# Where the split weights begin in SBUF: 96 bytes past a multiple of 128, in every stage

## The chip, the cores and the metric

The kernel runs on one core of a Trainium2 chip, one of the chip's eight. The metric is the device time in microseconds (us), the median of three runs. TensorE is called PE in the profile (its weight loads PEld), VectorE DVE, ScalarE ACT, GpSimd POOL and SyncE SP. SBUF is the on-chip memory from which TensorE reads both operands of a matmul; every tile has 128 partitions, and "address" below means the byte offset within a partition.

## The reference

One layer of a streaming encoder, over 256 tokens of 2048 features, all in float32. Cut to what matters:

```
x = x + hybrid_mixer(rmsnorm(x), w_in, ..., w_br, w_out)
x = x + memory_cross_attention(rmsnorm(x), rmsnorm(mem), xa_wq, xa_wkv, xa_wo, ...)
x = x + (silu(g) * u) @ ffn_down      # g, u = split(causal_conv3(rmsnorm(x) @ ffn_up))
```

The mixer has one wide input projection (h @ w_in), three token mixers (gated DeltaNet, mLSTM, stick-breaking attention), a projection of each by w_br, gates, and an output projection by w_out. Nearly all of the work is the dense products of 256 tokens with 367 MB of weights that are read once each.

## The kernel before, in words

A float32 product is made from three products of the faster type float32r. A weight w is split into hi = round(w) and lo = w - hi, the activations x likewise, and the product is hi·x_hi + hi·x_lo + lo·x_hi.

**Units.** The weights come as 177 units (`STREAM`), each of 256 output columns: 2048 x 256 values, or 1408 x 256 in the down projection (`DN`). SP loads a unit into one of two slots of `raw`. Each unit is handled in two halves. For each half ScalarE writes `w_hi` (`hi_half`, shown as L540), VectorE writes `w_lo` (`lo_half`, L1131), and TensorE multiplies (`half_unit`). `w_hi_home` and `w_lo_home` have two slots, one for each half, of 2048 + 64 float32r values (8448 bytes, 66 times 128). ScalarE may overwrite a slot once TensorE has used it (`half_used`), and TensorE waits for `lo_ready`.

**The kinds of stage**, which differ in what TensorE holds and what it streams:
- Feature-major (`FM`, and the branch projections `BR`): the held operand (stationary, loaded by LDWEIGHTS) is a 128 x 128 block of weights, and the streamed one (moving) is 256 tokens of activations. `three` issues three matmuls for each of 16 blocks: L1961, L1962, L1963.
- Token-major (`TM_`: stages BV, CV, V): the other way around. The held operand is a block of activations and the streamed one is 256 columns of weights. The same three lines.
- Up and down projection (`UP`, `DN`): weights are held. One matmul streams x_hi and x_lo together (two rows of 256, shown as 128x512; L1998 and L2473), and a second one streams x_hi against w_lo (L2000, L2474). Two matmuls for each block.

In the profile a matmul reads `bank<-moving,stationary`: `bank<-x_home,w_hi_home` holds weights, `bank<-w_hi_home,x_home` streams them. The type float32r is shown as f32 there. A matmul's weight load is the LDWEIGHTS instruction of the same line; the load for the next matmul runs beside the present one.

**Addresses.** Tiles lie one behind another in SBUF, in the order of the code. In the built program the homes begin at these addresses: `w_hi_home` 49280, `w_lo_home` 66176, `x_home` 83072, `act_hl` 130464, `mem_hl` 146848, `y_hl` 196000, `gw_hi` 196768, `gw_both` 204960. Taken modulo 128, both weight homes and `x_home` begin at 0, and all the others at 32. The kernel itself begins the activations 8 values (32 bytes) into `x_home`:

```
x_hl = x_home[:, 8:8 + 2 * KC * SEQ].rearrange("p (j k s) -> p j k s", j=2, k=KC)
```

Every step from one block to the next (512 or 1024 bytes, 8448 between slots) is a multiple of 128, so an operand keeps its place modulo 128 through a stage. This is what TensorE reads, in bytes past a multiple of 128:

| matmuls | moving | stationary | moving minus stationary |
|---|---|---|---|
| feature-major, branches, UP, DN (before) | 32 | 0 | 32 |
| token-major (before) | 64 | 32 | 32 |
| the small gate projection, L2119 and L2120 | 32 | 32 | 0 |

The gate projection multiplies the ten gate columns that belong to no unit: 32 matmuls on `gw_both` and `gw_hi`, of the same type and shape as the others (a 128 x 128 stationary operand, 256 columns moving), once at the start:

```
mm(bank[4][:, 0:SEQ], gw_both[:, k, :], x_hl[:, 0, k, :], start=k == 0, stop=False)
last = mm(bank[4][:, 0:SEQ], gw_hi[:, k, :], x_hl[:, 1, k, :], start=False, stop=k == KC - 1)
```

The order of the instructions on each engine is written out by hand, and semaphores join the engines.

Of the kernel before, what the change touches and what calls it, by code (L numbers as in the profile page):

```python
# [8 lines left out]
P = 128  # L9
SEQ, D = 256, 2048  # L10
TT = SEQ // P
KC = D // P
# [7 lines left out]
CW = 256  # L20
GDN_TAPS, FFN_TAPS = 4, 3
EPS = 1e-6
BIG = 1e30


C_A = 0
# [78 lines left out]
def shape_masks():  # L105
# [8 lines left out]
    incl = np.concatenate([r <= t, r <= c], 1)  # L114
    return np.concatenate([ident, upper, later] + levels + [np.where(strict, 0, -BIG), np.where(incl, 0, BIG)],
                          1).astype(np.float32)


def build_program(nc, T, out):
# [3 lines left out]
    with ctx:  # L123
        def sb(name, shape, dt=f32, stack=ctx):
            return stack.enter_context(nc.sbuf_tensor(name, shape, dt))
# [5 lines left out]
        raw = sb("raw", [P, 2, KC * CW])  # L131
        w_hi_home = sb("w_hi_home", [P, 2, KC * P + 64], f32r)
        w_lo_home = sb("w_lo_home", [P, 2, KC * P + 64], f32r)
        w_hi, w_lo = w_hi_home[:, :, 0:KC * P], w_lo_home[:, :, 0:KC * P]
        wt_hi, wt_lo = w_hi_home[:, :, 16:16 + KC * P], w_lo_home[:, :, 16:16 + KC * P]
        e_scope = ExitStack()
        x_back = sb("x_back", [P, KC, SEQ], f32, e_scope)
        o_tm = sb("o_tm", [P, TT, D], f32, e_scope)
# [257 lines left out]

        def split_out(tile, kind, half):
            if kind == TM_:
                return (wt_hi if tile is w_hi else wt_lo)[:, half, :]
            k = DG if kind == DOWN else KC  # L400
            return tile[:, half, 0:k * P].rearrange("p (k n) -> p k n", n=P)

# [125 lines left out]
        def up_bank(par, half):  # L528

            return bank[4 + 2 * par + half]  # L530
# [7 lines left out]
        def _(act):  # L538
# [3 lines left out]
            def hi_half(name, i, par, hp, half):  # L542

                act.wait_ge(raw_full[par], hp * 16 + 16)
                if not (isinstance(hp, int) and 2 * hp + par == 0):
                    act.wait_ge(half_used, hp * 4 + (2 * par + half - 1))
                copy(split_out(w_hi, kind_of[name], half), halves(raw, kind_of[name], half, par)).then_inc(hi_ready, 1)

            def hi_part(part, name, i, par, hp, half):

                if part == 0:
                    act.wait_ge(raw_full[par], hp * 16 + 16)
                    if name != "A":
                        act.wait_ge(half_used, hp * 4 + (2 * par + half - 1))
                ks = slice(part * (KC // 2), (part + 1) * (KC // 2))
                copy(split_out(w_hi, FM, half)[:, ks, :], halves(raw, FM, half, par)[:, ks, :]).then_inc(hi_ready if part else wp_h, 1)
# [135 lines left out]
            def first_weights(j, done):  # L692
                act.wait_ge(*((raw_full[0], 16) if j else (w0_in, 16)))
                ks = slice(j * (KC // 2), (j + 1) * (KC // 2))
                copy(split_out(w_hi, FM, 0)[:, ks, :], halves(raw, FM, 0, 0)[:, ks, :]).then_inc(done, 1)
# [1260 lines left out]
        def _(pe):  # L1956
            mm = nc.tensor.matmul

            def three(o, w, x, start, stop):

                mm(o, w[0], x[0], start=start, stop=False)  # L1961
                mm(o, w[0], x[1], start=False, stop=False)  # L1962
                return mm(o, w[1], x[0], start=False, stop=stop)  # L1963
# [14 lines left out]
            def half_unit(name, i, par, hp, half, acts, ready=None, passed=None, parts=None, ks=range(KC)):  # L1978

                kind = kind_of[name]  # L1980
                whole = hp * 4 + (2 * par + half + 1)
                pe.wait_ge(*((wp_l, parts) if parts else (lo_ready, whole)))
                if kind == TM_:
                    for k in range(KC // 2):
                        kk = half * (KC // 2) + k
                        w = [t[:, half, k * CW:(k + 1) * CW] for t in (wt_hi, wt_lo)]
                        for a in range(TT):
                            x = [acts[:, j, kk, a * P:(a + 1) * P] for j in range(2)]
                            last = three(bank[par + 2 * a][:, 0:CW], x, w, kk == 0, kk == KC - 1)
                else:  # L1990
                    cuts = (0, GH, GH + MH, KC) if kind == BR else (0, KC)
                    for k in range(KC if name == "UP" else 0):
                        if parts and k == KC // 2:
                            pe.wait_ge(lo_ready, whole)
                        if ready and k % ready[2] == 0:
                            pe.wait_ge(ready[0], ready[1] + k // ready[2] + 1)
                        o = up_bank(par, half)
                        mm(o[:, :].rearrange("p (j s) -> p j s", j=2), w_hi[:, half, k * P:(k + 1) * P], acts[:, :, k, :],  # L1998
                           start=k == 0, stop=False)
                        last = mm(o[:, SEQ:2 * SEQ], w_lo[:, half, k * P:(k + 1) * P], acts[:, 0, k, :], start=False, stop=k == KC - 1)  # L2000
                    for k in ks if name != "UP" else ():
                        if parts and k == KC // 2:
                            pe.wait_ge(lo_ready, whole)
                        if ready and k % ready[2] == 0:
                            pe.wait_ge(ready[0], ready[1] + k // ready[2] + 1)
                        g = sum(k >= c for c in cuts) - 1
                        w = [t[:, half, k * P:(k + 1) * P] for t in (w_hi, w_lo)]
                        last = three(bank[par + 2 * g][:, half * SEQ:(half + 1) * SEQ], w, [acts[:, j, k, :] for j in range(2)],
                                     k == cuts[g], k + 1 == cuts[g + 1])
                        if kind == BR and half and k + 1 in cuts[1:3]:  # L2010
                            last.then_inc(br_t, 1)
                        if passed is not None and k % 2 and k + 1 < KC:
                            last.then_inc(passed, 1)
                if ks[-1] == KC - 1:
                    last.then_inc(half_used, 1)

            def product_half(m, acts=x_hl, ready=None, passed=None, parts=None, ks=range(KC)):

                name, i, par, hp, half = half_of(m)
                if half == 0 and ks[0] == 0:  # L2020
                    wait_bank(name, i)
                half_unit(name, i, par, hp, half, acts, ready, passed, parts, ks)

            def project(name, acts, start=0, stop=None):
                def unit(i, par, hp):
                    wait_bank(name, i)
                    for half in range(2):
                        half_unit(name, i, par, hp, half, acts)

                stop = COUNT[name] if stop is None else stop  # L2030
                if start < 2:
                    each_unit(pe, name, unit, start, min(2, stop))
                each_unit(pe, name, unit, max(2, start), stop)
# [59 lines left out]
            for k in range(KC):  # L2093
# [8 lines left out]
                w = [t[:, 0, k * P:(k + 1) * P] for t in (w_hi, w_lo)]  # L2102
# [424 lines left out]
```

## Time and profile before

| | |
|---|---|
| median of 3 runs | 2003.33 us (2003.0 to 2004.33) |
| profiled execution, first to last instruction (span) | 2001.0 us |
| what the median has beyond that span | 2.3 us |
| PE busy | 1987.1 us (99%), 14790 matmuls |
| PE weight loads busy | 1895.9 us (95%) |
| DVE busy | 1216.1 us (61%) |
| ACT busy | 892.0 us (45%) |
| granted TensorE clock | 1.000 of full speed |

The page gives no time of the profiled execution apart from its span, so the sums are made against the span and the 2.3 us are added. Matmuls overlap in the pipeline: the duration in a row is that of one matmul from start to end, longer than the distance from one start to the next. The distance between starts, called the pace below, sets the time of a long run of matmuls. It is read from the first and last start of a group, or from start times in the timeline.

### The profile page before, as it was taken

The page shows a single profiled execution, that of the slowest core. Times are in us where ns is not written, and L with a number is a line of the kernel's source. Part 1 is how long each engine was busy: PE and PEld are TensorE (multiplying, and loading weights), DVE is VectorE, ACT ScalarE, POOL GpSimd, SP SyncE. Part 2 cuts the span into 40 slices and gives each one's busy share as a digit, 9 for nine tenths or more (in the row PEclk, how much of TensorE's full clock was granted, in tenths as well). Part 3 has the DMA queues.
Part 4 walks back from the last instruction along what each step waited for, and adds up shares of the span by engine and source line. Part 5 has one row for each costly group of instructions (what it writes and reads, how often), then busy time and mean ns, then how long its engine had stood idle before and what let it go on. Part 6 is the DMA issues. An engine that isn't in the chain of part 4 may idle for free.

```text
span 2001.0 us, 34706 instructions
## 1 busy us (share of the span) xinstructions
PE 1987.1 (99%) x14790; PEld 1895.9 (95%) x14790; DVE 1216.1 (61%) x1352; ACT 892.0 (45%) x877; POOL 40.5 (2%) x62
## 2 busy tenths in 40 slices
PE   8999999999999999999999999999999999999999
PEld 8999999999999999999999999988888888888888
DVE  5677645445454476576655345777777777754444
ACT  5445334434364343455434344544444444433333
POOL 1000100000000000000000000000000000000000
PEclk9999999999999999999999999999999999999999
DMA  8766754665557766565564456665656565566664
GB/s 268 220 192 195 226 159 143 198 200 166 182 174 247 243 198 223 169 194 186 178 199 129 139 168 198 212 208 171 207 171 206 173 204 174 177 205 223 185 203 134
DMA packets 356637, 382.65 MB, mean 191 GB/s; under 512 B 8144, under 2 KB 351604, under 8 KB 355124
## 3 DMA queue, kind: packets, MB, share of 16 engines
q1 hardware_dynamic: 350947, 353.36, 55.9%
q0 software_dynamic: 5584, 27.70, 4.0%
q8 instruction: 88, 1.44, 0.3%
q14 instruction: 18, 0.14, 0.0%
HBM read 367.47 MB, written 13.58 MB: 190 GB/s over the span
## 4 chain that ended last, share of the span: by engine, by line
PE 97%; DVE 1%; ACT 1%; DMA 0%; issue 0%; SPq 0%; DVEq 0%; ACTq 0%
PE bank L1961 18%; PE bank L1962 18%; PE bank L1963 18%; PE bank L1998 16%; PE bank L2000 8%; PE bank L2473 8%; PE bank L2474 4%; PE bank L2381 1%; PE bank L2400 1%; PE bank L2158 1%; DVE w_lo_home L1131 1%; ACT w_hi_home L540 0%; PE bank L2204 0%; PE bank L2061 0%; PE bank L2152 0%; DMA ident<-in_shape_masks 0%
## 5 line engine op out<-in xcount | busy, mean ns | idle before, releaser
L1131 DVE TENSOR_TENSOR w_lo_home<-raw,w_hi_home 128x2048 fp32r<-128x2048 f32 (+1 forms) x349 | 756.7, 2168 | 606.2 <-ACT w_hi_home L540 605.8
L540 ACT ACTIVATE w_hi_home<-raw 128x2048 fp32r<-128x2048 f32 (+2 forms) x359 | 645.0, 1798 | 1047.5 <-PE bank L1963 624.3
L1961 PE MATMUL bank<-x_home,w_hi_home 128*128 128x256 f32 x2304 | 648.1, 281 | 1.9 <-DVE w_lo_home L1131 1.9
L1962 PE MATMUL bank<-x_home,w_hi_home 128*128 128x256 f32 x2304 | 643.1, 279 | 0.0
L1963 PE MATMUL bank<-x_home,w_lo_home 128*128 128x256 f32 x2304 | 642.8, 279 | 0.0
L1998 PE MATMUL bank<-x_home,w_hi_home 128*128 128x512 f32 x1408 | 488.5, 390 | 0.1
L1961 PEld LDWEIGHTS bank<-x_home,w_hi_home 128*128 128x128 f32 x2304 | 433.1, 188 | 2.8 <-DVE w_lo_home L1131 1.4
L1962 PEld LDWEIGHTS bank<-x_home,w_hi_home 128*128 128x128 f32 x2304 | 433.2, 188 | 0.2
L1963 PEld LDWEIGHTS bank<-x_home,w_lo_home 128*128 128x128 f32 x2304 | 433.0, 188 | 0.0
L2000 PE MATMUL bank<-x_home,w_lo_home 128*128 128x256 f32 x1408 | 397.0, 282 | 0.0
L1998 PEld LDWEIGHTS bank<-x_home,w_hi_home 128*128 128x128 f32 x1408 | 264.2, 188 | 55.7 <-issue 0.4
L2000 PEld LDWEIGHTS bank<-x_home,w_lo_home 128*128 128x128 f32 x1408 | 266.1, 189 | 0.0
L2473 PE MATMUL bank<-act_hl,w_hi_home 128*128 128x512 f32 x704 | 245.2, 391 | 0.0
L2474 PE MATMUL bank<-act_hl,w_lo_home 128*128 128x256 f32 x704 | 198.5, 282 | 0.0
L2473 PEld LDWEIGHTS bank<-act_hl,w_hi_home 128*128 128x128 f32 x704 | 132.2, 188 | 27.6
L2474 PEld LDWEIGHTS bank<-act_hl,w_lo_home 128*128 128x128 f32 x704 | 133.1, 189 | 0.0
L1961 PE MATMUL bank<-w_hi_home,mem_hl 128*128 128x256 f32 x256 | 73.5, 287 | 0.0
L1865 DVE SCALAR_TENSOR_TENSOR tmp<-tmp,vec 128x254 f32<-128x254 f32 (+1 forms) x176 | 73.0, 476 | 0.0
L1961 PE MATMUL bank<-mem_hl,w_hi_home 128*128 128x256 f32 x256 | 71.8, 280 | 0.0
L1962 PE MATMUL bank<-mem_hl,w_hi_home 128*128 128x256 f32 x256 | 71.5, 279 | 0.0
L1962 PE MATMUL bank<-w_lo_home,mem_hl 128*128 128x256 f32 x256 | 71.5, 279 | 0.0
L1961 PE MATMUL bank<-y_hl,w_hi_home 128*128 128x256 f32 x256 | 71.5, 279 | 0.0
(315 smaller groups left out, 1942.4 us busy)
## 6 DMA issues: line engine op xcount, KB each, us to landing
raw<-in_w_in SPq DMA_DIRECT2D x52, 2048.0 KB, 8.4
raw<-in_ffn_up SPq DMA_DIRECT2D x44, 2048.0 KB, 8.0
raw<-in_ffn_down SPq DMA_DIRECT2D x32, 1408.0 KB, 6.6
raw<-in_xa_wkv SPq DMA_DIRECT2D x16, 2048.0 KB, 9.3
raw<-in_w_br SPq DMA_DIRECT2D x8, 2048.0 KB, 8.4
raw<-in_w_out SPq DMA_DIRECT2D x8, 2048.0 KB, 8.3
raw<-in_xa_wq SPq DMA_DIRECT2D x8, 2048.0 KB, 8.3
raw<-in_xa_wo SPq DMA_DIRECT2D x8, 2048.0 KB, 8.4
```

Source lines behind the costliest of these rows:

```text
L540: return nc.scalar.activation(out_, in_, func, **kw)
L1131: tt(split_out(w_lo, kind, half), halves(raw, kind, half, par), split_out(w_hi, kind, half).bitcast(f32), ALU.subtract).then_inc(lo_ready, 1)
L1865: ins = v.scalar_tensor_tensor(o, b, w, o, ALU.mult, ALU.add)
L1961: mm(o, w[0], x[0], start=start, stop=False)
L1962: mm(o, w[0], x[1], start=False, stop=False)
L1963: return mm(o, w[1], x[0], start=False, stop=stop)
L1998: mm(o[:, :].rearrange("p (j s) -> p j s", j=2), w_hi[:, half, k * P:(k + 1) * P], acts[:, :, k, :], start=k == 0, stop=False)
L2000: last = mm(o[:, SEQ:2 * SEQ], w_lo[:, half, k * P:(k + 1) * P], acts[:, 0, k, :], start=False, stop=k == KC - 1)
L2158: last = mm(o[:, i * P:(i + 1) * P], lhs(n), rhs(n), start=True, stop=True)
L2381: last = mm(mb(j)[:, 0:SEQ], qT[:, 4 * h + c, a * P:(a + 1) * P], kT[:, 4 * h + c, :], start=c == 0, stop=c == XC - 1)
L2473: mm(o[:, :].rearrange("p (j s) -> p j s", j=2), w_hi[:, half, k * P:(k + 1) * P], x, start=g + k == 0, stop=False)
L2474: last = mm(o[:, SEQ:2 * SEQ], w_lo[:, half, k * P:(k + 1) * P], x[:, 0, :], start=False, stop=g * DG + k == FC - 1)
```

## The change

The first value of every split-weight slot moves. In feature-major stages, branches, UP and DN, `w_hi` and `w_lo` began at 0 bytes of their slot; in token-major stages (`wt_hi`, `wt_lo`) at 64 bytes. Now all begin at 24 values, which is 96 bytes.

```
+W_AT = 24
...
-        w_hi, w_lo = w_hi_home[:, :, 0:KC * P], w_lo_home[:, :, 0:KC * P]
-        wt_hi, wt_lo = w_hi_home[:, :, 16:16 + KC * P], w_lo_home[:, :, 16:16 + KC * P]
+        w_hi, w_lo = (t[:, :, W_AT:W_AT + KC * P] for t in (w_hi_home, w_lo_home))
...
             if kind == TM_:
-                return (wt_hi if tile is w_hi else wt_lo)[:, half, :]
+                return tile[:, half, :]
...
-                        w = [t[:, half, k * CW:(k + 1) * CW] for t in (wt_hi, wt_lo)]
+                        w = [t[:, half, k * CW:(k + 1) * CW] for t in (w_hi, w_lo)]
```

The slots have room for it (24 + 2048 of 2112 values), no tile moves, and each engine's list of instructions is the same, row by row. What TensorE reads after the change, in bytes past a multiple of 128:

| matmuls | moving | stationary | moving minus stationary |
|---|---|---|---|
| feature-major, branches, UP, DN | 32 | 96 | -64, that is 64 modulo 128 |
| token-major | 96 | 32 | 64 |
| the gate projection | 32 | 32 | 0 |

## Rows read from the trace of the kernel before

**Rows 1.** The page's first part: engines, busy time, share, instructions.

```profile
PE 1987.1 (99%) x14790; PEld 1895.9 (95%) x14790; DVE 1216.1 (61%) x1352; ACT 892.0 (45%) x877; POOL 40.5 (2%) x62
```

**Rows 2.** Waits of PE, 20 to 1990 us: total, times, longest.

```profile
PE bank L1961 <- DVE w_lo_home L1131: 1.9, 3, 1.2
```

**Rows 3.** Waits of all engines, the whole span.

```profile
ACT w_hi_home L540 <- PE bank L1963: 624.3, 187, 6.4
DVE w_lo_home L1131 <- ACT w_hi_home L540: 605.8, 274, 7.2
```

**Rows 4.** Groups by line and shape: count, then busy us, mean ns of one, idle before.

```profile
L1961 PE MATMUL bank<-x_home,w_hi_home 128*128 128x256 f32 x2304 | 648.1, 281 | 1.9 <-DVE w_lo_home L1131 1.9
...
L1961 PE MATMUL bank<-w_hi_home,mem_hl 128*128 128x256 f32 x256 | 73.5, 287 | 0.0
L1961 PE MATMUL bank<-mem_hl,w_hi_home 128*128 128x256 f32 x256 | 71.8, 280 | 0.0
...
L1961 PE MATMUL bank<-y_hl,w_hi_home 128*128 128x256 f32 x256 | 71.5, 279 | 0.0
...
L1961 PE MATMUL bank<-w_hi_home,x_home 128*128 128x256 f32 x160 | 44.7, 279 | 0.0
```

**Rows 5.** Tile w_hi_home: min/median/max ns, first and last start us.

```profile
L1961 PE MATMUL bank<-y_hl,w_hi_home x256: 277/279/281, 684.2 to 773.4; 128*128 128x256 f32 x128
...
L1998 PE MATMUL bank<-x_home,w_hi_home x1408: 390/390/579, 1259.9 to 1748.9; 128*128 128x512 f32 x176
...
L2473 PE MATMUL bank<-act_hl,w_hi_home x704: 390/390/484, 1749.3 to 1996.2; 128*128 128x512 f32 x176
```

**Rows 6.** Timeline of PE, token-major, at 540 us: start us, duration us.

```profile
539.79 0.28 PE L1962 MATMUL bank<-w_lo_home,x_home 128*128 128x256 f32 x1
...
540.61 0.28 PE L1963 MATMUL bank<-w_hi_home,x_home 128*128 128x256 f32 x1
```

**Rows 7.** Timeline of PE, the gate projection, at 38 us.

```profile
37.83 0.28 PE L2120 MATMUL bank<-x_home,gw_hi 128*128 128x256 f32 x1
37.95 0.28 PE L2119 MATMUL bank<-x_home,gw_both 128*128 128x256 f32 x1
...
38.67 0.28 PE L2119 MATMUL bank<-x_home,gw_both 128*128 128x256 f32 x1
```

**Rows 8.** Tiles gw_both, then w_hi_home with y_hl, as in rows 5.

```profile
L2119 PEld LDWEIGHTS bank<-x_home,gw_both x16: 187/192/192, 36.2 to 39.7; 128*128 128x128 f32 x16
L2119 PE MATMUL bank<-x_home,gw_both x16: 278/283/283, 36.3 to 39.9; 128*128 128x256 f32 x16
...
L1961 PEld LDWEIGHTS bank<-y_hl,w_hi_home x256: 187/188/189, 684.1 to 773.3; 128*128 128x128 f32 x128
```

**Rows 9.** The longest pieces of the critical chain: start us, length us, what.

```profile
248.80 2.68 PE bank L2158 x24
...
1077.12 3.45 PE bank L2381 x16
```

**Rows 10.** Busy time in stretches: us, PE, PEld, DVE, ACT, POOL, clock, DMA.

```profile
700.00:750.00 50.00, 50.00 (x431) 50.00 (x431) 38.36 (x38) 20.42 (x14) 0.00 (x0) 1.00 0.62 196
1300.00:1400.00 100.00, 100.00 (x579) 88.67 (x578) 78.30 (x109) 44.07 (x45) 0.00 (x0) 1.00 0.59 189
37.20:39.60 2.40, 2.40 (x22) 2.40 (x21) 1.11 (x1) 1.25 (x1) 0.69 (x1) 1.00 1.08 372
```

**Rows 11.** Splitting, groups as in rows 4: first feature-major (700:760), then token-major (1060:1160).

```profile
L1131 DVE TENSOR_TENSOR w_lo_home<-raw,w_hi_home 128x2048 fp32r<-128x2048 f32 x11 | 25.2, 2289 | 13.0 <-ACT w_hi_home L540 13.0
...
L540 ACT ACTIVATE w_hi_home<-raw 128x2048 fp32r<-128x2048 f32 x11 | 21.1, 1918 | 35.4 <-PE bank L1963 35.4
...
L1131 DVE TENSOR_TENSOR w_lo_home<-raw,w_hi_home 128x2048 fp32r<-128x2048 f32 x13 | 29.7, 2286 | 16.6 <-ACT w_hi_home L540 16.6
...
L540 ACT ACTIVATE w_hi_home<-raw 128x2048 fp32r<-128x2048 f32 x13 | 24.9, 1913 | 47.3 <-PE bank L1963 47.3
```

## The prediction, made before the changed kernel ran

> **What bounds the kernel now.** I read the page's busy times first [rows 1]: TensorE is busy for 1987.1 of 2001.0 us, so only 13.9 us hold no matmul. Then the waits. From 20 to 1990 us TensorE waits for VectorE 1.9 us in all [rows 2], while ScalarE waits 624.3 us for TensorE to free a slot, and VectorE 605.8 us for ScalarE [rows 3]. So the splitting engines and the transfers have room, and the time is that of a row of matmuls. The granted clock is full in every stretch [rows 10], 2.4 GHz. What is left to change is how far apart two matmuls start.
>
> I read that pace next. In the branch stage the L1961 matmuls on y_hl start at 684.2 us first and at 773.4 us last, 256 of them [rows 5]. Between two of them lie three matmuls, so the pace is 89.2 / (255 x 3) = 116.6 ns. Token-major gives 0.82 us over seven starts, 117 ns [rows 6]. In the up projection a pair (512 and 256 columns) takes 489.0 / 1407 = 347.5 ns [rows 5]. In the down projection a pair takes 246.9 / 703 = 351.2 ns, a few transposes and the joins between column blocks included.
>
> The gate projection has the same type and shape, and it is slower: 37.83 to 38.67 us for seven starts [rows 7], 120.0 ns. Its matmuls last 283 ns and its loads 192 ns in the median, where the ordinary ones take 279 and 188 ns [rows 5, 8]. The clock is 1.00 there too [rows 10]. What distinguishes it in layout: its stationary operand begins 32 bytes past a multiple of 128, as the moving one does. Feature-major and token-major differ in both absolute places (32 over 0, 64 over 32), agree in the difference of 32, and run at one pace within what the rows resolve. The price of a layout can be read here, but at two layouts only, and the new one (difference 64) is neither.
>
> How much of the pace could layout touch? Two rows bound it. Plain float32 matmuls of 128 columns with a fresh weight load each run at 2.68 us / 24 = 111.7 ns, and those of 256 columns at 3.45 / 16 = 215.6 ns [rows 9]. That float32 streams its columns in two passes is an inference from the second: 512 steps at 2.4 GHz are 213.3 ns. One pass of 256 steps takes 106.7 ns. So our 116.6 ns has some 10 ns beyond streaming and 5 ns beyond the pace of loads in the nearest row.
>
> A rule speaks against any effect. The Trainium skill (TensorE: Matmul & The Clock Gate, Step-by-step: what each phase is for) says that TensorE has two independent SBUF read ports, and that loading the next weights takes no read bandwidth from the running matmul. By it, where one operand lies relative to the other would not matter, and the sum would be zero. This trace does not agree plainly: 120.0 against 116.6 ns at equal shape, type and clock is not what independent reads would give, unless the gate projection is slow for another reason.
>
> **The change part by part.**
> - *Stationary reads, feature-major, branches, UP, DN:* from 0 to 96 bytes past 128. The three-matmul kinds hold 2304 + 256 + 256 blocks with weights stationary; the token-major ones 256 + 160 with activations stationary [rows 4]. These are 3232 blocks and 9696 matmuls, some 1131 us at 116.6 ns. UP and DN have 1408 + 704 pairs [rows 5], 4224 matmuls. Together 13920.
> - *Moving reads, token-major:* from 64 to 96, the same new difference of 64 (1248 of the matmuls above).
> - *ScalarE and VectorE writes and VectorE's read:* moved likewise. ScalarE takes 1918 ns at 0 bytes and 1913 ns at 64, VectorE 2289 and 2286 [rows 11]. Their start does not show in their duration. I take nothing for 96 bytes. Matmuls of a half last 48 x 116.6 ns = 5.6 us, which hides both (4.2 us in sequence, and they overlap with the half before). If the cover were gone, even 5 ns on each of about 350 splits of either engine would be 3.5 us.
> - *DMA, semaphores, order:* nothing changes.
>
> Price of one matmul at difference 64. No row shows it. The nearest row with another layout is the gate projection: +3.4 ns (120.0 - 116.6), about 8 cycles of 2.4 GHz. From below the row of float32 loads bounds it: 111.7 - 116.6 = -4.9 ns, or -68 us in all. From above the only row for reads that don't overlap at all is the load's own 188 ns [rows 8], which would be +71 ns and 990 us; I don't believe that end, as the slower layout costs 3.4 ns.
>
> I choose +3.4 ns for every split-weight matmul. My reason is an even-granule view: 32 bytes past a multiple of 64 appears to cost 8 cycles on either operand. Feature-major has one such operand (the moving), token-major one (the stationary), the gate projection two, at 120.0. After the change 96 is again 32 past 64, so every matmul has two. This view gives the two equal paces and the slower one without more assumptions. The sum: 9696 x 3.4 ns = 33 us, and for UP and DN 4224 x 3.4 ns = 14 us (one shifted load per matmul, whatever its length). Together 47 us on the span of 2001.0, with 2.3 us around it: 2050 us. I put 2049 us (rounding 8 cycles to 3.33 ns gives 46).
>
> **The rivals.**
> - *Faster: the two reads take turns, and the wait falls with the difference.* With difference 0 the pace is 288 cycles, with 32 it is 280; in line with that 64 would give 272, 113.3 ns. Price -3.3 ns x 13920 = -46 us: 1957 us. For it: the two kinds of stage agree in the difference and in nothing else, and it stays above the 111.7 ns. Against: two points make any line, and it decides only if the difference and not the absolute place counts. Half the effect, 1980 us, is possible where only some stages respond.
> - *No change.* The gate projection is slow for a reason of its own: it alternates two tiles and two halves of x instead of reusing a tile. Then 2003 us. The sixteen-byte lines of SBUF that the Trainium skill describes (SBUF — State Buffer, Door 1: The DMA port swizzle) would say the same, as 0, 32, 64 and 96 are all multiples of 16. No row here shows lines of that size.
> - *Much slower: the difference counts, and 64 is its worst place.* If the pace rises on both sides of 32 and 64 costs twice what 0 does, 16 cycles or 6.7 ns, then 13920 x 6.7 = +93 us: 2096 us. For it: 0 is worse than 32. Against: it needs a step between 32 and 64 that no row shows.
> - *Only the three-matmul stages slow:* +33 us, 2036 us; in UP and DN half of the long matmul runs with no load beside it. Kept within the forecast's own range.
>
> **How the numbers follow.** Forecast, with its variant of 2036: 0.43. Much slower: 0.11. No change: 0.18. Faster: 0.28. So slower by over 0.2% has 0.54, within 0.2% 0.18, faster by over 0.2% 0.28; 0.2% (4 us) is about what a measurement of this kernel tells from no change. The forecast's own range is 2030 to 2058. The range of 8 in 10 runs from 1954, which takes in the faster rival, to 2062; it leaves out the much slower one and what lies below 1954.
>
> **What would show it.** If right: L1961 matmuls on y_hl span 91.8 us from first to last instead of 89.2 (120.0 ns), their median duration is 283 ns and that of their loads 192 ns; token-major steps by 0.12 us; a pair in UP takes about 354 ns; the gate projection keeps 120.0; DVE and ACT keep their durations and wait longer for TensorE. If the pace in those rows is 113 ns, the turn-taking rival holds and I have the sign wrong; if 116.6, the gate projection misled me. A pace that moves in feature-major and not in token-major would say that the held operand's absolute place counts. A longer wait of TensorE for VectorE, with an equal pace, would say that the price lies in the splitting, which I have at nothing.

## The result, and the profile after

The changed kernel takes 2009.08 us, the median of five runs from 2004.10 to 2014.77, against 2003.82 us (2003.0 to 2004.48) before. The ratio is 1.0031, with a 95% interval of 1.0020 to 1.0041: slower by 0.3%. The forecast was 2049 us. The spread is a result as well. These five runs of the kernel before lie within 1.5 us (thirteen measured with the first experiments within 3.0), those of the changed one within 10.7 us. The profiled execution, to which all rows below belong, is the fastest of the five: 2004.1 us with a span of 2002.1 us, 1.1 us above the span before.

The small sum hides two large parts of opposite sign. These rows of the tile w_hi_home answer to [rows 5] and [rows 8]; the columns are min/median/max ns, then the first and last start in us.

```profile
L1961 PEld LDWEIGHTS bank<-y_hl,w_hi_home x256: 187/188/188, 679.2 to 765.9; 128*128 128x128 f32 x128
L1961 PE MATMUL bank<-y_hl,w_hi_home x256: 276/276/276, 679.3 to 766.0; 128*128 128x256 f32 x128
...
L1998 PE MATMUL bank<-x_home,w_hi_home x1408: 389/397/581, 1247.4 to 1745.5; 128*128 128x512 f32 x176
...
L2473 PE MATMUL bank<-act_hl,w_hi_home x704: 392/397/481, 1745.9 to 1997.3; 128*128 128x512 f32 x176
```

The branch stage has become faster: 86.7 us from first to last start against 89.2, which is 113.3 ns a matmul against 116.6. UP starts at 1247.4 us instead of 1259.9, so everything ahead of it has gained 12.5 us. From there to the last L2473 start it takes 749.9 us instead of 736.3, a loss of 13.6 us. A pair in UP takes 498.1 / 1407 = 354.0 ns (347.5 before), in DN 251.4 / 703 = 357.6 (351.2). The sum is +1.1 us, the difference of the spans.

Not all stages of three matmuls gained. This is the timeline of PE at 644 us, in stage GC of the changed kernel: start us, duration us.

```profile
643.70 0.28 PE L1961 MATMUL bank<-x_home,w_hi_home 128*128 128x256 f32 x1
...
644.88 0.28 PE L1962 MATMUL bank<-x_home,w_hi_home 128*128 128x256 f32 x1
644.99 0.28 PE L1963 MATMUL bank<-x_home,w_lo_home 128*128 128x256 f32 x1
...
646.57 0.36 PE L1961 MATMUL bank<-x_home,w_hi_home 128*128 128x256 f32 x1 [1.29 <-DVE w_lo_home L1131]
646.76 0.28 PE L1962 MATMUL bank<-x_home,w_hi_home 128*128 128x256 f32 x1
...
647.12 0.28 PE L1962 MATMUL bank<-x_home,w_hi_home 128*128 128x256 f32 x1
...
647.91 0.28 PE L1963 MATMUL bank<-x_home,w_lo_home 128*128 128x256 f32 x1
```

The same lines, the same operands and the same places in memory run at 1.29 / 11 = 117 ns up to 644.99 us, then TensorE waits 1.3 us for a late unit, and from 647.12 on they run at 0.79 / 7 = 113 ns. I followed the start times of all three-matmul stages in blocks of twelve. Nearly every block after the change has one of two paces, 113.3 ns (272 cycles of 2.4 GHz) or 117.8 ns (282.7 cycles). Which of the two is settled within some twelve matmuls after a break, that is, after TensorE has waited or done other matmuls. It then stays through hundreds of matmuls, and it is the same while VectorE splits and while it is idle (113.3 ns either way in the branch stage), so the writes into the slots don't set it. Before the change nine blocks in ten had 116.7 ns (280 cycles).

TensorE need not wait for the pace to change. Here token-major BV passes into feature-major BO at 424.75 us with no gap:

```profile
423.39 0.28 PE L1961 MATMUL bank<-w_hi_home,x_home 128*128 128x256 f32 x1
...
424.75 0.28 PE L1961 MATMUL bank<-x_home,w_hi_home 128*128 128x256 f32 x1
...
426.16 0.28 PE L1961 MATMUL bank<-x_home,w_hi_home 128*128 128x256 f32 x1
```

Twelve steps take 1.36 us, then 1.41: 113.3 and 117.5 ns. So the passage from one kind of stage to the other counts as a break too.

| matmuls of the three-matmul stages, in whole blocks | 113.3 ns | 116.7 ns | 117.8 ns |
|---|---|---|---|
| before | 0 | 8136 | 864 |
| changed, first profile | 5400 | 24 | 3540 |
| changed, second profile (below) | 2580 | 12 | 6432 |

(Four blocks to a half; a block counts where nothing else lies among its twelve matmuls, by the mean of their eleven start distances: up to 114.5, up to 117.3, up to 120 ns. Blocks above that hold a break.) In the first profile 5400 x 3.3 ns = 17.8 us are gained and 3540 - 864 matmuls lose 1.1 ns each, 2.9 us: 15 us, of which 12.5 arrived. The longer wait for VectorE below is 1.3 us of the rest.

The other predicted readings, in the order of the groups. Token-major, at 540 us, seven steps take 0.80 us (539.82 to 540.62), 114 ns. The wait of TensorE for VectorE from 20 to 1990 us is 3.2 us instead of 1.9 [rows 2]:

```profile
PE bank L1961 <- DVE w_lo_home L1131: 3.2, 3, 1.3
```

ScalarE waits less for the three-matmul stages, 604.0 us instead of 624.3 [rows 3]; I had forecast a longer wait:

```profile
ACT w_hi_home L540 <- PE bank L1963: 604.0, 184, 6.4
```

The windows, with the columns of [rows 10] (this is the row of UP, 1300 to 1400 us): the clock is as before, and in UP 569 matmuls touch the 100 us where 579 did. The gate projection and the splitting are unchanged [rows 8, 11]:

```profile
1300.00:1400.00 100.00, 100.00 (x569) 86.87 (x568) 76.75 (x105) 43.55 (x45) 0.00 (x0) 1.00 0.58 188
```

```profile
L2119 PE MATMUL bank<-x_home,gw_both x16: 283/283/283, 36.4 to 40.0; 128*128 128x256 f32 x16
```

```profile
L1131 DVE TENSOR_TENSOR w_lo_home<-raw,w_hi_home 128x2048 fp32r<-128x2048 f32 x12 | 27.5, 2289 | 13.7 <-ACT w_hi_home L540 13.7
```

### The profile page after: what moved, and what is told of

Its sections match the earlier page's. It is cut to its first block, busy times and chain, and to the rows that moved or that the text cites. A ratio compares the mean times of both kernels' runs of the same rounds, so it can differ in the third digit from the quotient of the medians.

```text
span 2002.1 us, 34706 instructions
## 1 busy us (share of the span) xinstructions
PE 1987.0 (99%) x14790; PEld 1880.8 (94%) x14790; DVE 1216.2 (61%) x1352; ACT 892.4 (45%) x877; POOL 40.4 (2%) x62
## 4 chain that ended last, share of the span: by engine, by line
PE 96%; DVE 2%; DMA 1%; ACT 1%; issue 0%; SPq 0%; DVEq 0%; ACTq 0%
PE bank L1961 18%; PE bank L1962 18%; PE bank L1963 18%; PE bank L1998 17%; PE bank L2000 8%; PE bank L2473 8%; PE bank L2474 4%; DMA raw<-in_w_in 1%; DVE w_lo_home L1131 1%; PE bank L2381 1%; PE bank L2400 1%; PE bank L2158 1%; ACT w_hi_home L540 0%; PE bank L2204 0%; PE bank L2061 0%
## 5 line engine op out<-in xcount | busy, mean ns | idle before, releaser
L540 ACT ACTIVATE w_hi_home<-raw 128x2048 fp32r<-128x2048 f32 (+2 forms) x359 | 645.3, 1799 | 1045.7 <-PE bank L1963 604.0
L1961 PE MATMUL bank<-x_home,w_hi_home 128*128 128x256 f32 x2304 | 646.3, 280 | 3.4 <-DVE w_lo_home L1131 3.2
L1998 PE MATMUL bank<-x_home,w_hi_home 128*128 128x512 f32 x1408 | 497.9, 398 | 0.0
L1961 PEld LDWEIGHTS bank<-x_home,w_hi_home 128*128 128x128 f32 x2304 | 435.3, 189 | 4.8 <-issue 2.9
L1998 PEld LDWEIGHTS bank<-x_home,w_hi_home 128*128 128x128 f32 x1408 | 264.7, 188 | 65.5 <-issue 0.2
L2473 PE MATMUL bank<-act_hl,w_hi_home 128*128 128x512 f32 x704 | 249.7, 398 | 0.0
L2473 PEld LDWEIGHTS bank<-act_hl,w_hi_home 128*128 128x128 f32 x704 | 132.4, 188 | 32.4
L1961 PE MATMUL bank<-w_hi_home,mem_hl 128*128 128x256 f32 x256 | 73.3, 286 | 0.0
L1963 PE MATMUL bank<-w_hi_home,mem_hl 128*128 128x256 f32 x256 | 71.3, 279 | 0.0
L1961 PE MATMUL bank<-mem_hl,w_hi_home 128*128 128x256 f32 x256 | 71.0, 277 | 0.0
L1963 PE MATMUL bank<-mem_hl,w_lo_home 128*128 128x256 f32 x256 | 70.7, 276 | 0.0
```

The costliest lines, as they stand in the source:

```text
L540: return nc.scalar.activation(out_, in_, func, **kw)
```

## The experiments

From here on a difference is the moving operand's address minus the stationary one's, in bytes, as a signed value modulo 256 (the homes of the weights begin 128 past a multiple of 256, all activations 160). Before: +32 everywhere. Changed: -64, and +64 in token-major stages. The expectations of the first two kernels and the first two maps count modulo 128. In a table of places, W_AT gives where a stage's weights begin, in columns of 4 bytes: with the activations at 32 bytes and the weights held, 0 is +32, 24 is -64. All kernels but the repeat of the changed one are the kernel before with a table of places, one for each stage, and keep its line numbers. Their tables are written in short form below, stages and then their place:

```
-        w_hi, w_lo = w_hi_home[:, :, 0:KC * P], w_lo_home[:, :, 0:KC * P]
-        wt_hi, wt_lo = w_hi_home[:, :, 16:16 + KC * P], w_lo_home[:, :, 16:16 + KC * P]
+        w_hi, w_lo, kind_of = w_hi_home, w_lo_home, {n: k for n, _, _, _, k in STREAM}
+        placed = lambda tile, name: tile[:, :, W_AT[name]:W_AT[name] + KC * P]
...
```

### One part at a time

```
+W_AT = 24 in every stage but UP and DN, 0 there
```

> Weights begin at 96 bytes in all stages of three matmuls, and again at 0 in the up and down projection. Theory D (the pace is set by moving minus stationary, modulo 128; at 64 a run of matmuls settles at either 113.3 or 117.8 ns and keeps that until it is broken): the pairs of UP and DN go back from 353.5 to 346.7 ns, which gives back 1408 x 6.8 + 704 x 6.8 = 14.4 us against the changed kernel, and the rest keeps the 13 us gained in its profiled execution or less: 1988 to 1999 us, varying from run to run by up to 10 us. Rival G (something in the whole program, for instance the transfers, takes back what the matmuls gain): 2003 us or more.

Measured: 1999.62 us, nine runs from 1995.84 to 2001.08; ratio to before 0.9972 (0.9962 to 0.9982). UP takes the old time, 489.0 us from first to last start of L1998:

```profile
L1961 PEld LDWEIGHTS bank<-y_hl,w_hi_home x256: 192/192/192, 677.7 to 767.8; 128*128 128x128 f32 x128
L1961 PE MATMUL bank<-y_hl,w_hi_home x256: 281/281/281, 677.8 to 767.9; 128*128 128x256 f32 x128
...
L1998 PE MATMUL bank<-x_home,w_hi_home x1408: 390/390/579, 1257.6 to 1746.6; 128*128 128x512 f32 x176
```

The branch stage, whose places are those of the changed kernel, has 90.1 us here, 117.8 ns. The duration of these loads tells the two paces apart as well: 192 ns here, 188 ns there. (It is one of the three loads of a block that lengthens, and not in every stage that of L1961.) Rival G falls, and the median lies just above the 1988 to 1999 us of theory D. The profiled execution is the slowest of the nine, 2001.08 us; it has 2676 matmuls at 113.3 ns and 6324 at 117.8.

```
+W_AT = 24 in UP and DN; elsewhere as before (0, token-major 16)
```

> The reverse: only UP and DN hold weights at 96 bytes, all the rest as before. Theory D: each pair takes 353.5 ns, +14.4 us, 2018 us, with no more variation from run to run than the kernel before, because the two-state stages are unchanged. Rival G: less than 10 us of it shows.

Measured: 2017.38 us (2016.70 to 2017.77), ratio 1.0067 (1.0053 to 1.0081), and L1998 spans 498.1 us. Theory D holds in both: the loss is 13.6 us (14.4 expected), and the spread is gone, 1.1 us. Rival G falls here too. UP and DN carry the whole loss, the other stages the gain and the spread.

### The same kernel once more

> The changed kernel once more, to see whether the two paces belong to places in the program or to the execution. Theory D: each unbroken run of matmuls settles anew, so other stages are at 113.3 and at 117.8 ns than in the first profile (there the branches ran at 113.3 and XO at 117.8), and the span differs by up to 10 us; UP and DN are at 353.4 ns a pair again. Rival C (the place in the program decides, for instance what runs before): the same stages at the same paces, and the branches at 113.3.

Measured: 2014.59 us in one run, span 2012.6 us.

```profile
L1961 PE MATMUL bank<-y_hl,w_hi_home x256: 281/281/281, 678.1 to 768.2; 128*128 128x256 f32 x128
...
L1998 PE MATMUL bank<-x_home,w_hi_home x1408: 392/397/581, 1257.8 to 1756.0; 128*128 128x512 f32 x176
```

The branch stage is at 117.8 ns in this execution. Everything ahead of UP has gained 2.1 us instead of 12.5, and UP and DN lose as in the first profile. Rival C falls as stated: the same place in the program can run at either pace. But the place has a large share in it. Z, BQK, BV and CV ran at 113.3 ns in all three profiles with these places, BO and XO at 117.8. Counted by halves, this profile and that of the kernel with UP and DN put back, taken on another chip, have the same pace in 196 of 200; the first profile agrees with this one in 120 of 199, and the others lie mostly from GB to V. What decides at a break, and how much of it is chance, stays open.

### Maps of places

Each map is one run of a kernel that gives each stage another place, and I read the pace of each stage from start times. As wholes the four maps took 2029.65, 2022.15, 2018.53 and 2008.75 us, one run each.

```
+W_AT = A 0, Z GA BV DN 8, BQK BO CQK UP 16, CV Q 24, GB GC 28, BR 20, WO 12, K 4, V 0, XO 26
```

> A map: each stage gets a place of its own for its weights, the activations stay at 32 bytes past 128. Differences (moving minus stationary, modulo 128): A 32; Z and GA 0; BV (token-major) 0; BQK, BO and CQK 96; CV (token-major) 64; GB and GC 48; BR 80; WO 112; K 16; Q 64; V (token-major) 96; XO 56; UP 96; DN 0. Theory D: GA, and BV with it, run at 120.0 ns like the gate projection; CV at 113.3 or 117.8; A at 116.7; K between 116.7 and 120. Rival P (each operand's own place counts, 32 past 64 costing 8 cycles): GA 120.0, but BQK, BO and CQK (64 stationary, 32 moving) 116.7, and V (0 moving, 32 stationary) 116.7. Rival N (the gate projection was slow for a reason of its own): GA at 116.7.

```
+W_AT = GA Q 0, CQK CV 8, A Z BV GB GC WO UP DN 16, BR 22, BQK BO K V XO 24
-        x_hl = x_home[:, 8:8 + 2 * KC * SEQ].rearrange("p (j k s) -> p j k s", j=2, k=KC)
+        x_hl = x_home[:, 0:0 + 2 * KC * SEQ].rearrange("p (j k s) -> p j k s", j=2, k=KC)
```

> The same kind of map with the activations of the feature-major stages at 0 instead of 32 bytes past 128. Differences: A and Z 64 (0 over 64); GA and Q 0 (0 over 0); BQK, BO 32 (0 over 96); BV 64 (64 over 0); CQK 96; CV 32 (32 over 0); GB and GC 64 (0 over 64); BR 72; WO 64; K and V 64 (as in the changed kernel); XO 32; UP 64 (0 over 64); DN 96. Theory D: GA and Q at 120.0 ns though both operands begin at a multiple of 128; BQK, BO, XO and CV at 116.7; A, Z, GB, GC, WO at 113.3 or 117.8, and a pair in UP at 353.5. Rival P: GA and Q are the fastest, 113.3 ns, as nothing is off a multiple of 64, and so are A, GB and WO, always.

```
+W_AT = XO 24, A GA WO V UP 32, CQK K 40, BV Q 48, Z BQK BO CV GB GC BR DN 56
```

> A map to find what the difference is taken modulo of, activations at 32 past 128 (all 160 past a multiple of 256; the weight homes begin 128 past 256). Differences in bytes, moving minus stationary, given as signed values modulo 256: A, GA, WO and UP -96; Z, BQK, BO, GB, GC, BR, DN +64 (weights at 224 of the slot, before only -64 was run); CQK and K 128; BV -96; CV -64; Q +96; V +96; XO -64 (control). Theory D128 (only modulo 128 counts): A, GA, WO at 116.7 ns and pairs of UP at 346.7, since -96 is 32 modulo 128; CQK and K at 120.0; Z to BR at 113.3 or 117.8; pairs of DN 353.4. Theory D256 (the difference counts modulo 256 or more; the map with x at 0 had -96 in BQK, BO and XO at 117 to 119 and not at 116.7): A, GA, WO at 117 to 119, UP at 353.4, CQK and K not at 120.0.

```
+W_AT = A Z BQK BO CV GB GC WO Q UP 0, BR 2, DN 6, GA XO 8, BV CQK 24, K V 56
-        x_hl = x_home[:, 8:8 + 2 * KC * SEQ].rearrange("p (j k s) -> p j k s", j=2, k=KC)
+        x_hl = x_home[:, 16:16 + 2 * KC * SEQ].rearrange("p (j k s) -> p j k s", j=2, k=KC)
```

> A map with the activations of the feature-major stages at 64 past 128. Signed differences modulo 256: A, Z, BQK, BO, GB, GC, WO, Q and UP +64 (64 over 0); GA and XO +32 (64 over 32, weights held); BV +32 (96 over 64); CQK -32; CV -64; BR +24; K +64; V -64; DN +8. Theory D: GA and XO run at 116.7 ns as at 32 over 0. +64 is like -64 if only the distance counts: 113.3 or 117.8, and 353.4 for a pair in UP. Rival S (the sign counts: the moving read ahead of the load by 64 goes on from what +32 does to 0): +64 at 113.3 ns always and pairs in UP below 346.7.

What the four maps and the kernels above gave, by difference:

| difference | ns a matmul (stages of three) | where (moving over stationary, modulo 128) |
|---|---|---|
| 0 | 120.0 | GA, Z, BV (32 over 32); GA, Q (0 over 0) |
| +16 | 117 to 120 | K (32 over 16) |
| +24 | 117.5 to 118 | BR (fourth map) |
| +32 | 116.7, at times 117.8 | 32 over 0, 64 over 32, 32 over 0 token-major |
| +64, -64 | 113.3 or 117.8 | 0 over 64, 64 over 0, 96 over 32, 32 over 96 and others |
| +96 | 120.0 | Q, V |
| 128 | 118 to 120 | CQK, K |
| -96 | 117 to 119, a part of WO 120.0 | A, GA, WO, BV (32 over 0); BQK, BO, XO (0 over 96) |
| -80 to -16, without -64 | 118 to 119, a part of WO 120.0 | GB, GC, XO, BR, BQK, CQK, WO, V |

Two rows each of the timeline of PE decide between theories: in the first map Z (32 over 32), in the second Q (0 over 0), in the fourth XO (64 over 32).

```profile
133.82 0.28 PE L1961 MATMUL bank<-x_home,w_hi_home 128*128 128x256 f32 x1
...
134.78 0.28 PE L1963 MATMUL bank<-x_home,w_lo_home 128*128 128x256 f32 x1
```

```profile
999.83 0.28 PE L1963 MATMUL bank<-x_home,w_lo_home 128*128 128x256 f32 x1
...
1000.79 0.28 PE L1962 MATMUL bank<-x_home,w_hi_home 128*128 128x256 f32 x1
```

```profile
1199.76 0.28 PE L1963 MATMUL bank<-x_home,w_lo_home 128*128 128x256 f32 x1
...
1200.69 0.28 PE L1962 MATMUL bank<-x_home,w_hi_home 128*128 128x256 f32 x1
```

Eight steps take 0.96 us in the first two, 120 ns, and 0.93 in the third, 116 ns. So:
- Rival N falls: ordinary matmuls at difference 0 run at 120.0 ns. The gate projection was a true sample; with the activations at 0 or 64 it runs at 117.0 itself.
- Rival P, which is the view my forecast rested on, falls: with both operands at a multiple of 128 the pace is 120.0 ns, the slowest, and not the fastest.
- Theory D holds in what it says of the difference: 64 over 32 is as 32 over 0, and 0 over 0 as 32 over 32. It falls in the modulus. -96 and +32 are equal modulo 128, but GA at -96 takes 117 to 119 ns. The difference counts modulo 256 at least. No larger modulus shows: the two halves of a unit lie 8448 bytes apart, which is 256 modulo 512, and run alike (GA of the first map at 120.0 ns in both halves, the branch stage of the kernel before at 116.6).
- Rival S falls: +64 has the same two paces as -64.

For the pairs of UP and DN the maps follow another pattern. The table has the mean inside a half, without the joins that the 347.5 ns of [rows 5] include:

| | hi, lo difference | ns a pair, UP or DN |
|---|---|---|
| before, e1 | +32, +32 | 346.7 |
| third map, UP | -96, -96 | 346.7 |
| fourth map, UP | +64, +64 | 349.0 |
| third map, DN | +64, +64 | 352.4 |
| fourth map, DN | +8, +8 | 351.7 |
| changed, e2 | -64, -64 | 353.3 |
| first map | UP -32, DN 0 | 352.9, 353.4 |
| second map | UP -64, DN -32 | 353.3, 353.3 |

(e1 is the kernel with UP and DN put back, e2 the one with only these two changed.) The third map's UP has the old time, 1271.5 to 1760.5 us. There theory D256, which holds for the stages of three matmuls, missed and D128 was right; in the fourth map UP at +64 took 349.0 ns, where theory D had 353.4:

```profile
L1998 PE MATMUL bank<-x_home,w_hi_home x1408: 391/392/584, 1271.5 to 1760.5; 128*128 128x512 f32 x176
```

### High and low halves apart

A second table places `w_lo`:

```
+        placed = lambda tile, name: (lambda at: tile[:, :, at:at + KC * P])((W_LO if tile is w_lo else W_AT)[name])
+(W_AT, W_LO) = A GA CV WO DN (24, 0), Z GC V (24, 16), BQK CQK Q UP (0, 24),
+               BV BO GB K (24, 56), BR (24, 8), XO (56, 24)
```

> The high and the low halves of the weights get places of their own, written (hi, lo) as signed moving minus stationary in bytes: A, GA, WO (-64, +32); Z, GC (-64, -32); BQK, CQK, Q (+32, -64); BV (+64, -64 with 224 of 256); BO, GB, K (-64, +64); CV (+64, -32); BR (-64, 0); V (+64, +32); XO (+64, -64); UP (+32, -64); DN (-64, +32). Theory B (what counts is the load that runs beside a matmul, against what this matmul streams): in UP the load of lo runs beside the matmul of 512 columns, so UP (+32, -64) shows 235 + 118 ns, as with both at -64; in DN the load of lo lies at +32 and the long matmul takes 228, while the load of hi beside the short one lies at -64 and costs nothing, 346.7 a pair. Rival A (each matmul's own operands count, whatever loads beside it): the other way around, UP 228 + 118 and DN 235 + 118. In the stages of three matmuls I have no number for mixtures: between 113.3 and 118; if one of them holds 113.3 ns after every break, it is the version to time.

```profile
L1998 PE MATMUL bank<-x_home,w_hi_home x1408: 388/393/586, 1266.5 to 1755.5; 128*128 128x512 f32 x176
L2473 PE MATMUL bank<-act_hl,w_hi_home x704: 392/396/481, 1755.9 to 2005.7; 128*128 128x512 f32 x176
...
L1961 PE MATMUL bank<-mem_hl,w_hi_home x256: 276/276/468, 872.8 to 960.0; 128*128 128x256 f32 x128
```

One run, 2012.58 us. Theory B falls: UP has the old time, 489.0 us, with its low halves at -64, and DN (high halves at -64) is slow, 351.1 ns a pair. Among the mixtures one stands out. High at -64 with low at +64 gave 113.3 ns in BO, GB and K, in every block away from a break (in K the L1961 matmuls on mem_hl span 87.2 us, in the kernel before 89.9 by the same view). The reverse in XO gave 118.9, and no other mixture came below 116.7.

```
+(W_AT, W_LO) = every feature-major and branch stage (24, 56); BV CV V (24, 24); UP DN (0, 0)
```

> From the map of places for hi and lo apart: the high halves at 96 bytes, the low ones at 224 (24 and 56 values; differences -64 and +64) in all feature-major and branch stages; both at 96 in the token-major stages; both at 0 in UP and DN. In the map BO, GB and K with these places ran at 113.3 ns after every break. If this holds elsewhere (theory L: with the low halves 128 bytes further on, the 117.8 state can't be kept), some 8300 feature-major matmuls gain 3.3 ns, 27 us, and the token-major ones up to 4 us: 1974 to 1980 us with little variation. If the three stages had luck (theory R: two states as before), 1990 to 2000 us, varying. Where TensorE runs faster than the weights come, a few us go to waits for them.

Measured: 1976.43 us, four runs from 1976.03 to 1978.45, against 2003.66 (2003.31 to 2004.11); ratio 0.9867 (0.9851 to 0.9884). The span of the profiled execution is 1973.9 us.

```profile
L1961 PE MATMUL bank<-y_hl,w_hi_home x256: 276/276/276, 669.3 to 756.0; 128*128 128x256 f32 x128
...
L1961 PE MATMUL bank<-mem_hl,w_hi_home x256: 276/276/468, 848.1 to 935.4; 128*128 128x256 f32 x128
L1961 PE MATMUL bank<-w_hi_home,mem_hl x256: 276/279/468, 1024.6 to 1143.7; 128*128 128x256 f32 x128
...
L1998 PE MATMUL bank<-x_home,w_hi_home x1408: 390/390/579, 1232.9 to 1722.0; 128*128 128x512 f32 x176
```

All feature-major and branch stages run at 113.3 ns after every break. UP starts 27.0 us earlier than before, at 1232.9 us, and UP and DN take the old time. Only V, token-major and with both halves at +64, still has the two paces (119.1 us, 118.9 in the kernel before). Theory L holds for the feature-major and branch stages. This kernel is 1.3% faster than the kernel before, by the medians 1.6% faster than the changed one, and its four runs lie within 2.4 us.

```
+the same, with UP (0, 56), DN (0, 24), BV CV V (56, 24)
```

> The kernel with 96 and 224 bytes once more, with other places in four kinds of stage, (hi, lo) as signed moving minus stationary: UP (+32, +64), DN (+32, -64), token-major V, BV and CV (-64, +64). If each matmul's own operands count in the pairs, as UP (+32, -64) at 346.7 ns and DN (-64, +32) at 351 said, both UP and DN are at 346.7 here; if the load beside the long matmul counts, at 353.4. Token-major: no number, 113.3 if the mixture of signs does there what it does feature-major. The feature-major stages again at 113.3 (theory L) or in two states (theory R).

```profile
L1961 PE MATMUL bank<-x_home,w_hi_home x2304: 276/276/469, 16.7 to 1235.4; 128*128 128x256 f32 x192
...
L1998 PE MATMUL bank<-x_home,w_hi_home x1408: 388/397/579, 1235.8 to 1733.7; 128*128 128x512 f32 x176
L2473 PE MATMUL bank<-act_hl,w_hi_home x704: 388/393/481, 1734.1 to 1980.9; 128*128 128x512 f32 x176
```

One run, 1987.65 us. Feature-major stages are at 113.3 ns again, a second execution. The token-major ones ran at 117.8 ns. The pairs did not follow either rule: UP (+32, +64) took 353.0 ns, DN (+32, -64) 346.7. That "each matmul's own operands count" is thereby refuted for UP, and what sets a pair's pace stays open.

## Why the prediction was wrong

- **What bounds the kernel, and that the pace depends on the places: right.** Clock, order, splitting and transfers did not change; the price is in the distance between matmul starts, and the gate projection was a fair sample of another layout [rows 7]. Its own pace goes from 120.0 to 117 ns when its activations move by 32 bytes, in either direction. The Trainium skill (TensorE: Matmul & The Clock Gate, Step-by-step: what each phase is for) has weights and data read over independent ports. These runs don't agree that where one lies relative to the other is without effect: 120.0 ns at a difference of 0, 116.7 at 32. What the two reads share is not shown.
- **The price of a matmul at the new difference: the step that failed.** I wrote +3.4 ns for each of 13920 matmuls, by the view that every operand 32 past a multiple of 64 costs 8 cycles. It fitted all three layouts that I had, and so did the difference, which I gave to a rival. 0 over 0 at 120.0 ns refutes the view. In place of +3.4 ns the 9696 matmuls of the three-matmul stages have -3.3 ns or +1.1 ns, and which of them settles anew at each break. The term of +33 us measured -12.5 us in one execution and -2.1 in another.
- **UP and DN: the size was right by luck, the reason not.** I had 14 us as 3.4 ns on each of 4224 matmuls. Measured 13.6 us (changed) and the same in the kernel with only this part. But all of it lies on the long matmul: from its start to the next one it takes 235.2 ns instead of 228.5 in the mean of UP, and the short one keeps 118. Also a difference of 0 costs a pair what -64 does (353.4 and 353.3 ns).
- **The faster rival** had the right pace, 113.3 ns, and the right reason in part: the difference counts and not the place. It took the pace for certain, and it extended the gain to UP and DN, where the loss is. I named "half the effect, where only some stages respond", but not a loss in the others.
- **The sign** is what I forecast, at a ninth of the size: +5.3 us on the medians instead of +46. It comes out of UP and DN alone. Had the other stages lost as well, the kernel with UP and DN put back would not be faster than the kernel before. The range of 1954 to 2062 held the time because of the rivals, not because of the forecast.
- **Missed:** that one layout can have two paces, and so that the change would widen the spread from 1.5 to 10.7 us. The trace before held a sign of it: 864 of its matmuls ran at 117.8 ns with the places of the others.

## What to carry to other kernels

Where matmuls with a fresh weight load each bound a kernel, read the distance between their starts for each stage and compare it with the columns streamed. If some cycles are over, the offset between the two operands is worth a map: one kernel with another offset in each stage shows a dozen of them in one profile. Choose by stage, since matmuls of 256 and of 512 columns wanted different places here (the best kernel gained 27 us and the uniform one lost 5). And profile a layout more than once, because a fast pace in one profile may be one of two.

## What the runs showed of the hardware

- A stream of float32r matmuls of 256 columns, each with its own load of 128 columns, started every 113.3 to 120.0 ns (272 to 288 cycles at a full clock), depending on the distance of its two operands in SBUF, modulo 256 bytes. All distances tried are multiples of 8 bytes.
- At a distance of 64 bytes either way, two paces are stable, 113.3 and 117.8 ns. The one taken is kept for hundreds of matmuls and settles anew when TensorE waits, runs other matmuls or passes from one kind of stage to another. In part the place in the program decides it (196 of 200 halves alike in two profiles), in part something that differs between executions. In the branch stage the load of L1961 lasts 188 ns at the fast pace and 192 at the slow one.
- With a difference of -64 bytes for the high halves and +64 for the low ones, only the fast pace remained in feature-major and branch stages, in two executions of whole kernels and in three stages of another. The reverse order gave 118.9 ns, and token-major the mixture gave 117 to 118. Pairs of matmuls of 512 and 256 columns took 346.7 to 353.4 ns by another pattern, which I can't put into a rule. Why is open: the runs show what the offsets do, not which part of the read path they meet.
